# Prompt attention of a hybrid decoder step: scores issued three units ahead, and exponentials and copies alternating by head on ScalarE

## The reference, cut to what matters

```
def masked_softmax(s, valid):
    s = jnp.where(valid, s, NEG_INF)
    e = jnp.exp(s - jnp.max(s, axis=-1, keepdims=True)) * valid
    return e / jnp.maximum(jnp.sum(e, axis=-1, keepdims=True), 1e-30)

def gqa_attend(q, k, v, dist, valid, slopes):
    s = jnp.einsum('...tgrd,...kgd->...grtk', q, k) * (HEAD_DIM ** -0.5)
    s = s - slopes[:, :, None, None] * dist[..., None, None, :, :]
    p = masked_softmax(s, valid[..., None, None, :, :])
    return jnp.einsum('...grtk,...kgd->...tgrd', p, v), p

o = gates[..., 0:1] * o_cmp + gates[..., 1:2] * o_slc + gates[..., 2:3] * o_win
```

## Time and profile before

| | us |
|---|---|
| median of 3 runs (lowest, highest) | 2483.07 (2475.38, 2487.23) |
| the profiled execution | 2482.11 |
| its span in the trace | 2480.3 |
| granted TensorE clock, mean over the span | 0.883 |
| TensorE, VectorE, ScalarE, GpSimd busy, whole span | 2002.2, 850.2, 672.4, 732.2 |

### The profile page before, as it was taken

The page is one execution under the profiler, slowest core; times in us unless marked ns, Lnnn a source line. Parts: engine busy times, 40 slices in busy tenths (PEclk is TensorE's granted clock), DMA queues, the critical chain, the costliest instruction groups (busy, mean ns, idle before and its releaser), DMA issues. The chain is left out here.

```text
span 2480.3 us, 46089 instructions
## 1 busy us (share of the span) xinstructions
PE 2002.2 (81%) x20699; PEld 1807.2 (73%) x20699; DVE 850.2 (34%) x1196; ACT 672.4 (27%) x972; POOL 732.2 (30%) x332
## 2 busy tenths in 40 slices
PE   6985775466678999997968886888666689999978
PEld 6974445344467999997948884888624679999968
DVE  2014332244423311312262214666298433113131
ACT  3221551144423312312222213222101233223121
POOL 2300000054442443432212221333262223443422
PEclk9986886577789999998978887999887799999989
DMA  4106763610011222222111100000210112222210
GB/s 163 52 1 212 224 194 119 211 46 1 1 52 68 86 105 92 86 103 68 52 52 68 52 20 11 4 4 4 78 49 9 68 52 98 99 86 103 86 52 35
DMA packets 93139, 183.73 MB, mean 74 GB/s; under 512 B 11615, under 2 KB 70887, under 8 KB 78991
## 3 DMA queue, kind: packets, MB, share of 16 engines
q1 hardware_dynamic: 92942, 180.79, 21.6%
HBM read 164.52 MB, written 16.25 MB: 73 GB/s over the span
## 5 line engine op out<-in xcount | busy, mean ns | idle before, releaser
L251 POOL TENSOR_TENSOR ws_t<-ring,ws_t 128x2048 fp32r<-128x2048 f32 x74 | 340.1, 4597 | 615.4 <-ACT ws_t L245 615.4
L228 PE MATMUL P<-uh,ws_t 128*128 128x260 f32 x2560 | 420.5, 286 | 35.0 <-DVE ul L264 35.0
L228 PEld LDWEIGHTS P<-uh,ws_t 128*128 128x128 f32 x2560 | 357.9, 191 | 37.7 <-issue 35.0
L228 PE MATMUL P<-hidh,ws_t 128*128 128x260 f32 x2176 | 350.9, 283 | 0.0
L228 PEld LDWEIGHTS P<-hidh,ws_t 128*128 128x128 f32 x2176 | 299.1, 188 | 0.0
L228 PE MATMUL P<-ul,ws_t 128*128 128x260 f32 x1280 | 260.9, 286 | 0.0
L1373 POOL TENSOR_SCALAR S_<-S_,st_ 128x128 f32<-128x128 f32 (+3 forms) x96 | 102.2, 1082 | 459.0 <-DVE st_ L1410 459.0
L245 ACT ACTIVATE ws_t<-ring 128x2048 fp32r<-128x2048 f32 x74 | 141.5, 1914 | 301.5 <-PE P L228 301.5
L228 PE MATMUL P<-hidl,ws_t 128*128 128x260 f32 x1088 | 218.9, 283 | 0.0
L228 PEld LDWEIGHTS P<-ul,ws_t 128*128 128x128 f32 x1280 | 200.1, 191 | 0.0
L228 PEld LDWEIGHTS P<-hidl,ws_t 128*128 128x128 f32 x1088 | 167.2, 188 | 0.0
(11 more groups left out here) (352 smaller groups left out, 3517.4 us busy)
## 6 DMA issues: line engine op xcount, KB each, us to landing
ring<-in_weights SPq DMA_DIRECT2D x104, 1024.0 KB, 4.7
ring<-in_rows SPq DMA_DIRECT2D x32, 384.0 KB, 4.5
raw<-in_rows SPq DMA_DIRECT2D x32, 384.0 KB, 4.7
vs<-in_cv_slc SPq DMA_DIRECT2D x64, 128.0 KB, 2.2
vw<-in_win_v SPq DMA_DIRECT2D x8, 512.0 KB, 4.3
out_win_v<-vw SPq DMA_DIRECT2D x8, 512.0 KB, 8.4
out_kv<-Z SPq DMA_DIRECT2D x1, 3120.0 KB, 10.8
xn<-in_win_k SPq DMA_DIRECT2D x12, 256.0 KB, 4.9
```

The source lines that it names most:

```text
L228: mm = pe.matmul(P[:, n // 2 % 2 * 4 + 2 * m + hf, 0:HT], w, xs[:, i * nk + k, hf * HT:(hf + 1) * HT], start=first_k and w is wh and xs is xh,
L251: pool.tensor_tensor(ws[:, u % 2, 1, :], ring[:, u % RING, :], ws[:, u % 2, 0, :].bitcast(F32), ALU.subtract).then_inc(wsplit_ready, 1)
```

## The change

TensorE begins with the scores of three units instead of two, and in iteration u issues scores(u+3) instead of scores(u+2); the order inside an iteration (scores, turn 0, values, turn 1) stays. On ScalarE the loop over the two heads now stands outside: two exponentials of head 0 of u, the copy of turn (u-2, 0), two exponentials of head 1 of u, the copy of turn (u-2, 1). `e_done` steps once for each head instead of once for each unit, and VectorE's normaliser waits for twice the count.

```diff
-                        scores(0)
-                        scores(1)
+                        for u in range(3):
+                            scores(u)
                         for u in range(NUN + 1):
-                            if u + 2 < NUN:
-                                scores(u + 2)
+                            if u + 3 < NUN:
+                                scores(u + 3)
                             if u < NUN:
                                 turn(u, 0)
...
                     def _(act):
                         for u in range(NUN + 2):
-                            if u < NUN:
-                                act.wait_ge(m_ready, u + 1)
-                                n = width(u)
-                                for g2 in range(2):
+                            for g2 in range(2):
+                                if u < NUN:
+                                    act.wait_ge(m_ready, u + 1)
+                                    n = width(u)
                                     for b in range(2):
                                         j = 2 * b + g2
                                         x = S[:, u % SB, j, 0:n]
                                         mm = act.activation(x, x, ACT.Exp, bias=st[:, u % SB, 0, j:j + 1],
                                                             accum_out=st[:, u % SB, 1, j:j + 1])
-                                mm.then_inc(e_done, 1)
-                            if u >= 2:
-                                v = u - 2
-                                n = width(v)
-                                if v >= 2:
-                                    act.wait_ge(o_done, v - 1)
-                                for g2 in range(2):
+                                    mm.then_inc(e_done, 1)
+                                if u >= 2:
+                                    v = u - 2
+                                    n = width(v)
+                                    if v >= 2:
+                                        act.wait_ge(o_done, v - 1)
                                     act.wait_ge(t_done, 2 * v + g2 + 1)
                                     act.activation(PT[:, v % 2, 2 * g2:2 * g2 + 2, 0:n], P[:, 4:6, 0:n], ACT.Copy)\
                                        .then_inc(t_copied, 1)
...
-                                dve.wait_ge(e_done, v + 1)
+                                dve.wait_ge(e_done, 2 * v + 2)
```

## The result

The changed kernel takes 2399.8 us (median of four runs, 2393.2 to 2403.9) against 2480.8 before: ratio 0.9662, interval 0.9643 to 0.9681. Measured again later beside the kernel before, 0.9656 (0.9634 to 0.9678). The direction and the mechanism were as forecast; the gain (81 us by the medians, 84 by the ratio, 85.5 by the spans of the two profiles) was larger than the 72 of the sum.

What follows compares the result with a forecast made beforehand. Prompt attention was taken as bound by a ring of waits closed within one unit, no engine full. Gains of 15.5 (fill), 54.4 (four laps) and 2 (end), together 72 us, take 2482.1 to 2410; range 2398 to 2442.

Steps and rivals of the forecast that it cites:

- The bound: Prompt attention: no engine full; a ring of waits closed within one unit, in a lap of 34.11 us.
- The walk: New lap of four units followed engine by engine from scores of 512 keys: 19.0 us at full clock.
- I take the middle, near 0.92: TensorE's granted clock in the new lap, between 0.86 and 1.00 seen elsewhere; makes the lap 20.5 us.
- the four laps: Middle of the prompt attention stage, up to unit 23's scores: each lap 34.1 to 20.5 us, gain 54.4.
- the fill: Start of the stage, up to unit 7's scores: first lap 25.7 us, gain 15.5 (bounds 9 and 22).
- the end: From unit 23's scores to the stage's last copy: 25.5 us falls to 23.3, gain 2.
- The low clock (1): TensorE's clock does not rise: 2428 us at 0.75 (chance 0.14 as now or somewhat better), 2466 at 0.50 (low, 0.06).
- the rule on transposes: Skill page: transposes don't count for TensorE's clock gate; 5.5 of 17.2 us of work would not hold the clock.
- The lost lead (2): Bias-add starts no earlier relative to its copy, only halved exponentials count: lap 29.7, 2455 us; chance 0.07.
- The full buffer of four slots: S buffer: bias-add of u+3 waits for turn(u-1,1), which precedes scores(u+3) on TensorE; adds nothing.
- The second ring (3): Ring through VectorE and GpSimd binds longer than walked: 2422 us, or 2432 if all of it; chance 0.10.
- Exclusion (4): VectorE's bias-add and maxima and GpSimd's scaling exclude each other: lap 36, 2492 us, slower; chance 0.03.

Runs made afterwards that it cites:

- the repeat: The full change, unaltered, measured once more beside the kernel before: 2398.0 us, ratio 0.9656.
- the other order: The full change with the units of a lap in the order 128, 512, 384, 256 keys instead of rising: 2398.7 us, ratio 0.9673.
- both omissions: The full change with the sliding branch neither scaled on GpSimd nor multiplied with its values on TensorE: lap 18.79 us.

## Where the prediction was right, and the step that failed

**The bound** was read rightly: a ring over scores, maxima, exponentials and copy, closed within one unit. Either half of the change alone loosens it, and the waits that made it are gone from the list.

**The walk** of the new lap gave 19.0 at the full clock; it is 18.83, with the starts listed above within 0.2 us.

**The step that failed** is the clock: "I take the middle, near 0.92", which made 20.5 of 19.0. The laps ran at 1.00. The mechanism was right; this term was mis-sized. Term by term, the four laps gained 61.4 and not 54.4; the fill 17.9 and not 15.5 (unit 7's scores start 47.2 us into the stage before, 29.3 after), since the first lap was 22.9 at a clock of 0.78 and not 25.7; the end 1.8 for 2. The sum is 81 for 72. That the end agrees is luck: in the repeat it lasts longer than the 25.5 us before, partly at the low level:

```profile
594.72:620.93 26.21, 20.34 (x181) 14.94 (x180) 7.17 (x16) 11.73 (x25) 15.89 (x15) 0.80 0.00 1
```

Taken from 2482.1, the stage's 81 alone give 2401, inside the range. The other 4.5 us by which the spans differ lie outside the stage, where the prediction put nothing ("the gain reaches the end whole"); their cause is open, as said above.

The 0.92 came from two stretches elsewhere that were as busy, and a busy share with a mean clock beside it was the wrong thing to carry over. The stretch granted 0.86, in its parts, and TensorE's wait in it, in the kernel before:

```profile
1300.00:1311.90 11.90, 9.86 (x39) 8.51 (x39) 6.66 (x10) 3.15 (x5) 0.00 (x0) 0.50 0.01 1
1311.90:1356.30 44.40, 39.66 (x330) 39.45 (x329) 1.68 (x1) 11.96 (x12) 16.06 (x4) 1.00 0.20 72
1356.30:1362.00 5.70, 2.38 (x9) 2.11 (x10) 4.87 (x4) 0.73 (x2) 2.27 (x1) 0.50 0.38 137
PE P L228 <- DVE xml L264: 10.1, 7, 7.7
```

The low level at its end began inside the one wait of 7.7 us (1351.6 to 1359.3). The longer part, at its start, was brought along from before the stretch: low since 1294.9, right behind a gap of 2.0 us, though TensorE was 83% busy from 1300 on. So the 0.86 says little of a lap that is 92% busy with no gap above 1.02 us. Nor is "after TensorE had stood still 6 us" the whole of it: in the lap of the earlier trace rows the low level began inside that gap, at 612.2, not behind it.

What would have given the clock these runs show only in part. Laps between the first and the end whose longest gap is at most 1.04 us (the change in both profiles, and the runs with 240 transposes, half the scaling, the gap filled, the other order, maxima by head and both of these) all ran at 1.00. Of twelve with one gap of 2.1 to 2.5 us (the lead alone, values left out, both omissions) eleven ran at 0.76 to 0.92, and one at 1.00. But alternation alone ran at 0.94 with a gap of 4.7 us in the lap, and lead four at 0.87 and at 1.00 with gaps of up to 1.6 in either lap. So the longest gap alone doesn't give the clock either, and no rule for it is shown.

**The rivals.** The low clock (1) did not come, and the rule on transposes that it leaned on did not hold in the run with 240 of them. The lost lead (2) is what alternation alone looks like, 27.6 to 30.4 where 29.7 was worked out. The full buffer of four slots is no limit: over the whole stage the list of VectorE's waits has scores, exponentials and the last values, but no turn. A fifth slot with more lead is worse. The second ring (3) is as long as walked: the last turn waits 0.16 us for the scaling, and only both rings shortened together move the lap by more than 0.4. Exclusion (4) is not seen where it was to show: the scalings last 596 to 1572 ns, before 600 to 1565, the bias-adds 276 to 689, before 279 to 689. Only the first small instruction of the normaliser grew, from a median of 159 ns and at most 170 to 210 and 458; with GpSimd's work halved it is 170 and 171 again. Most of VectorE's 0.7 us more a lap is that; its cause is not shown. Two sums of the rivals are some 1 us off (9 + 6.4 is 15.4, not 16, in the first; all of the wait in the third leaves 49, not 50), and nothing hangs on them.

## What to carry to other kernels

When no engine is full, write down the ring of waits and count over how many units it closes: one unit more of lead took this lap from 34.1 us to 21.1, and with the alternation to 18.8, but a second unit more closed another ring (24.0), by the trace through the bank that the leading engine asks for. Then walk the new lap at the full clock. Its clock did not follow here from the busy share of other stretches; a gap of about 2 us in the walk is a risk to be priced, not a rule. Work taken from TensorE can be paid back by its clock if it leaves a gap: both omissions gave nothing until the gap was filled.

## What the runs showed of the hardware that was not expected

In the two kernels whose laps have one gap over 1 us, of 2.11, the granted clock was 0.91 in six laps, 0.76 in one and 1.00 in one. Filling the gap with 1.53 us of transposes that nobody reads, in the kernel with both omissions, brought 1.00 in every such lap and a lap 1.17 us shorter. Rows of transposes alone raised the clock from 0.50 to 1.00.
